# Block-diagonal queries: attention scores as full 128-row matmuls, with one layout buffer per mixer

## What is computed

```python
qa, ka, va, za, qb, kb, vb, zb, ga, gb = jnp.split(rms_norm(h, g_in) @ w_in, cuts, axis=-1)
# mixer A: 8 query heads, 2 key heads of 64; a chunk of 64 sees itself and the 2 chunks before
# mixer B: 8 query heads, 8 key heads of 64; a chunk sees itself and the 8 chunks before
s = jnp.einsum('bnqhgd,bnkhd->bnhgqk', qg, k) * (dh ** -0.5)
s = s + bias.reshape(Hkv, G, Cq, Kn)          # distance penalty (A) or learned table (B)
...                                           # mask, sink (A), softmax
o = jnp.einsum('bnhgqk,bnkhd->bnqhgd', pr, v)
branch_a = (oa * jax.nn.silu(za)) @ w_o_win
branch_b = (ob * jax.nn.silu(zb)) @ w_o_band
h = h + (jax.nn.sigmoid(ga) * branch_a + jax.nn.sigmoid(gb) * branch_b) @ w_out
gate = jax.nn.sigmoid(rms_norm(h, g_ple) @ w_ple_gate)
h = h + gate * (p @ w_ple)
```

## Time and profile before

| what | value |
|---|---|
| median of 3 runs | 1305.68 us (1210.99, 1305.68, 1320.73) |
| the profiled execution | 1209.5 us, span of the slowest core 1207.9 us |
| spans of the eight cores | 1203.1 to 1207.9 us |
| mean granted TensorE clock of the cores | 0.993 to 0.996 |
| busy: TensorE, VectorE, ScalarE, GpSimd | 96%, 60%, 54%, 39% of the span |
| DMA traffic of the slowest core | 106.84 MB, mean 88 GB/s |

### The profile page before, as it was taken

How to read it: one execution, slowest core, us unless ns; L and a number is a source line. 1 busy time by engine, 2 the same in 40 slices (tenths; PEclk the granted TensorE clock), 3 DMA queues, 4 the chain that set the end, 5 groups by cost and what they waited for, 6 DMA issues and landing times.

```text
span 1207.9 us, 22110 instructions; the slowest of 8 cores (1203.1 to 1207.9 us)
## 1 busy us (share of the span) xinstructions
PE 1156.1 (96%) x8119; PEld 569.9 (47%) x8275; DVE 723.9 (60%) x1671; ACT 650.8 (54%) x997; POOL 471.8 (39%) x516
## 2 busy tenths in 40 slices
PE   5799999999999999999999999999999999999896
PEld 2455554444444444444444444444444444444442
DVE  2765756556566655566566555565656556766654
ACT  2676554555555455555555555555555555655452
POOL 3743223433344433443444333443444334544520
PEclk9899999999999999999999999999999999999998
DMA  9999412333343334333443333333433344444463
GB/s 177 211 179 173 87 47 72 58 75 59 74 86 81 76 81 82 75 70 64 81 87 78 78 82 78 78 66 66 83 85 76 77 86 92 100 70 90 86 80 90
DMA packets 170252, 106.84 MB, mean 88 GB/s; under 512 B 149024, under 2 KB 154272, under 8 KB 167680
## 3 DMA queue, kind: packets, MB, share of 16 engines
q1 hardware_dynamic: 152608, 71.30, 25.6%
q0 software_dynamic: 17536, 34.12, 17.8%
HBM read 80.56 MB, written 21.50 MB: 84 GB/s over the span
## 4 chain that ended last, share of the span: by engine, by line
PE 91%; DMA 2%; DVE 2%; issue 2%; POOL 1%; ACT 1%; DVEq 0%; ACTq 0%; SPq 0%; POOLq 0%
PE psmm L203 81%; PE pss L203 6%; PE pso L203 5%; DMA xb<-xe 2%; POOL st L190 1%; DVE st L190 0%; DVE qkn L190 0%; DVE xb L190 0%; DVE psmm L190 0%; DVE scr L190 0%; DVE stq L190 0%; DVE ET L190 0%; DMA actT<-mbuf 0%; ACT ET L190 0%; ACT t1t L190 0%
## 5 line engine op out<-in xcount | busy, mean ns | idle before, releaser
L203 PE MATMUL psmm<-W_in,xT 128*128 128x512 bf16 (+1 forms) x2726 | 633.1, 370 | 11.8 <-issue 7.6
L203 PEld LDWEIGHTS psmm<-W_in,xT 128*128 128x128 bf16 x2848 | 251.7, 98 | 251.7 <-issue 12.0
L190 POOL TENSOR_TENSOR st<-st,mhalf 128x8 f32<-128x8 f32 (+1 forms) x174 | 227.6, 1313 | 164.5 <-DVE st L190 161.1
L190 ACT ACTIVATE ET<-pss 128x1024 bf16<-128x1024 f32 (+1 forms) x220 | 221.5, 1007 | 124.2 <-PE pss L203 122.1
L190 ACT ACTIVATE tg<-psmm,st 128x512 bf16<-128x512 f32 x132 | 90.1, 687 | 168.1 <-PE psmm L203 168.1
L190 POOL TENSOR_TENSOR zs<-ont,zs 128x256 bf16<-128x256 f32 (+1 forms) x132 | 89.5, 678 | 216.3 <-DVE ont L190 216.2
L203 PE MATMUL psmm<-W_pg,actT 128*128 128x512 bf16 x515 | 122.2, 386 | 4.9 <-DVE qkn L190 3.0
L203 PE MATMUL psmm<-W_out,actT 128*128 128x512 bf16 x521 | 120.3, 379 | 1.8 <-ACT actT L190 0.7
L190 ACT ACTIVATE scr<-psmm 128x512 f32<-128x512 f32 (+1 forms) x137 | 70.4, 517 | 66.3 <-PE psmm L203 44.9
L190 DVE TENSOR_TENSOR ET<-ET,tabAs 128x1024 bf16<-128x1024 bf16 (+1 forms) x66 | 44.8, 679 | 97.4 <-ACT ET L190 96.5
L190 DVE SCALAR_TENSOR_TENSOR psmm<-t1t,psmm 128x512 f32<-128x512 f32 x66 | 43.0, 693 | 94.5 <-PE psmm L203 94.5
(11 more groups left out here) (104 smaller groups left out, 1237.4 us busy)
## 6 DMA issues: line engine op xcount, KB each, us to landing
y<-xb SPq DMA_DIRECT2D x32, 512.0 KB, 2.6
xb<-xm SPq DMA_DIRECT2D x29, 512.0 KB, 3.9
W_in<-w_in POOLq DMA_DIRECT2D x10, 1024.0 KB, 27.0
xT<-xmT POOLq DMA_DIRECT2D x28, 256.0 KB, 3.9
xb<-xe POOLq DMA_DIRECT2D x2, 1536.0 KB, 13.6
pT<-pmT POOLq DMA_DIRECT2D x32, 64.0 KB, 2.4
W_out<-w_out POOLq DMA_DIRECT2D x2, 1024.0 KB, 63.0
W_pg<-w_pg POOLq DMA_DIRECT2D x2, 1024.0 KB, 59.2
```

Source lines behind the costliest of these rows:

```text
L190: inst = getattr(e, method)(*[_res(a_) for a_ in args], **{k_: _res(a_) for k_, a_ in kw.items()})
L203: last = getattr(e, m)(*[_res(a_) for a_ in a], **{k_: _res(a_) for k_, a_ in k.items()})
```

## The change

Queries are laid out block-diagonally. The staging area's columns 0 to 1023 are now shared by q of mixer A and q of mixer B, one after the other: each head pair takes 256 columns, of which the first and the last 64 hold the two heads and the 128 between them stay zero from one memset at the start. Transposed, a pair gives 128 partitions by 256 columns: one head on rows 0 to 63 of the first 128 columns, the other on rows 64 to 127 of the second 128, zeros elsewhere. With these the scores of two heads (mixer B) or four (mixer A) come from one matmul over all 128 rows of the key layout: mixer A has two of 512 columns, mixer B four of 256. qaT and qbT have 1024 columns and a single buffer each. Each mixer's q is transposed right after its multiply, so tiles on the TensorE path have 16 q blocks to transpose instead of 8. The order of heads in the exp buffers and in the tables changes with it, and at the start q of tile 1 is projected after the attention of tile 0 has been handed to the scheduler.

```diff
-    qaT = [sb(f"qaT{i}", [128, 512], BF16) for i in range(2)]
-    qbT = [sb(f"qbT{i}", [128, 512], BF16) for i in range(2)]
+    qaT = sb("qaT", [128, 1024], BF16)
+    qbT = sb("qbT", [128, 1024], BF16)
+    QR = ["qkn_q0", "qkn_q1"]
...
+    S.ins("dve", "memset", qkn[:, 0:1024], 0.0, w=QR, est=0.5)
...
-            o_ap = dst.rearrange("p (i kv d) -> p kv i d", kv=2, d=64)
-            i_ap = bank[:, c0:c0 + w].rearrange("p (kv i d) -> p kv i d", kv=2, d=64)
+            o_ap = dst.rearrange("p (i a d) -> p a i d", a=4, d=64)[:, 0:4:3]
+            pat = "kv i" if permute == "A" else "i kv"
+            i_ap = bank[:, c0:c0 + w].rearrange(f"p ({pat} d) -> p kv i d", kv=2, d=64)
...
+        def p_trq(dst_, dres):
             if t["dmaT"]:
-                for (off, w_, src_, dst_, dres) in (
-                        (0, 512, "qkn_qa", qaT[par][:], f"qaT{par}"), (1024, 128, "qkn_ka", kaT[:, sa, :], f"kaT{sa}"),
-                        (512, 512, "qkn_qb", qbT[par][:], f"qbT{par}"), (1152, 512, "qkn_kb", kbT[:, sbn, :], f"kbT{sbn}")):
-                    dmaT(dst_, qkn[:, off:off + w_], [src_], [dres])
+                dmaT(dst_[:], qkn[:, 0:1024], QR, [dres])
+                return
+            trx, trres = next_tr()
+            S.group("pe", [("transpose", (trx[:, c * 128:(c + 1) * 128], qkn[:, c * 128:(c + 1) * 128], ident[:]), {})
+                           for c in range(8)], r=QR + ["ident"], w=[trres])
+            S.ins("act", "copy", dst_[:], trx[:, 0:1024], r=[trres], w=[dres], est=1.0)
+
+        def p_trk():
+            if t["dmaT"]:
+                dmaT(kaT[:, sa, :], qkn[:, 1024:1152], ["qkn_ka"], [f"kaT{sa}"])
+                dmaT(kbT[:, sbn, :], qkn[:, 1152:1664], ["qkn_kb"], [f"kbT{sbn}"])
...
+                if "k" not in parts:
+                    bank, br = inproj_ct(t, 0, 512)
+                    qknorm(t, bank, br, 0, 8, qkn[:, 0:1024], QR, 0, permute="A")
+                    p_trq(qaT, "qaT")
+                if "Q" not in parts:
+                    p_a()
+                if "k" not in parts:
+                    bank, br = inproj_ct(t, 1280, 512)
+                    qknorm(t, bank, br, 0, 8, qkn[:, 0:1024], QR, 10, permute="B")
+                    p_trq(qbT, "qbT")
+                if "Q" not in parts:
+                    p_k()
+                    p_v()
+                    p_trk()
...
-                    sl = kt % RB_
-                    for hq in range(4):
-                        for hh in range(2):
-                            calls.append(("matmul", (ps_s[:, hh * 512 + hq * NQ:hh * 512 + (hq + 1) * NQ],
-                                                     kbT[hh * 64:(hh + 1) * 64, sl, hq * 128:(hq + 1) * 128],
-                                                     qbT[par][hh * 64:(hh + 1) * 64, hq * 128:hq * 128 + NQ]),
-                                          dict(start=True, stop=True)))
-                    S.group("pe", calls, r=[f"kbT{sl}", f"qbT{par}"], w=["pss0"], est=0.4)
+                sl = kt % (RA_ if mixer == "A" else RB_)
+                for g in range(2 if mixer == "A" else 4):
+                    nb_ = 4 if mixer == "A" else 2
+                    o_ = g * 512 if mixer == "A" else (g // 2) * 512 + (g % 2) * 2 * NQ
+                    lhs = kaT[:, sl, :] if mixer == "A" else kbT[:, sl, g * 128:(g + 1) * 128]
+                    rhs = (qaT if mixer == "A" else qbT)[:, g * nb_ * 128:(g + 1) * nb_ * 128]
...
+                    calls.append(("matmul", (ps_s[:, o_:o_ + nb_ * NQ], lhs, rhs), dict(start=True, stop=True)))
...
+                S.group("pe", calls, r=kr, w=["pss0"], est=0.45)
...
-    P(m[1], "q")
+    P(m[1], "qk")
     tabs_setup()
     P(m[0], "z")
     A(m[0])
+    P(m[1], "qQ")
     P(m[1], "z")
```

More of the change, by code:

```diff
@@ L605, in qknorm @@
         if permute:
-            o_ap = dst.rearrange("p (i kv d) -> p kv i d", kv=2, d=64)
-            i_ap = bank[:, c0:c0 + w].rearrange("p (kv i d) -> p kv i d", kv=2, d=64)
-            r_ap = rs.rearrange("p (kv i) -> p kv i", kv=2).unsqueeze(3).to_broadcast([128, 2, 4, 64])
-            S.ins("dve", "tensor_tensor", out=o_ap, in0=i_ap, in1=r_ap, op=ALU.mult, r=[bres, rsr], w=[dst_res],
+            o_ap = dst.rearrange("p (i a d) -> p a i d", a=4, d=64)[:, 0:4:3]
+            pat = "kv i" if permute == "A" else "i kv"
+            i_ap = bank[:, c0:c0 + w].rearrange(f"p ({pat} d) -> p kv i d", kv=2, d=64)
+            r_ap = rs.rearrange(f"p ({pat}) -> p kv i", kv=2).unsqueeze(3).to_broadcast([128, 2, 4, 64])
+            S.ins("dve", "tensor_tensor", out=o_ap, in0=i_ap, in1=r_ap, op=ALU.mult, r=[bres, rsr], w=dst_res,
                   est=0.15 + w / 950.0)
@@ L691, in p_tr @@
                 return
[L692 to L705, removed]
+            trx, trres = next_tr()
+            c_lo = 0 if needa else 1
+            S.group("pe", [("transpose", (trx[:, c * 128:(c + 1) * 128], qkn[:, 1024 + c * 128:1152 + c * 128], ident[:]), {})
+                           for c in range(c_lo, 5)], r=(["qkn_ka"] if needa else []) + ["qkn_kb", "ident"], w=[trres])
+            if needa:
+                S.ins("act", "mul", kaT[:, sa, :], trx[:, 0:128], gcol[:, 1:2], r=[trres, "gcol"], w=[f"kaT{sa}"], est=0.36)
+            S.ins("act", "mul", kbT[:, sbn, :], trx[:, 128:640], gcol[:, 3:4], r=[trres, "gcol"], w=[f"kbT{sbn}"], est=0.69)
         if "x" in parts:
@@ L714, in stage_P @@
                     p_a()
-                p_tr(True, False)
+                p_trk()
             else:
[L717 to L724, removed]
+                if "k" not in parts:
[11 more added lines that the diff above has]
+                    p_v()
+                    p_trk()
         if "z" in parts and full:
@@ L799, in stage_A @@
                 calls = []
-                if mixer == "A":
-                    sl = kt % RA_
-                    for hh in range(2):
[L803 to L807, removed]
-                    sl = kt % RB_
-                    for hq in range(4):
-                        for hh in range(2):
-                            calls.append(("matmul", (ps_s[:, hh * 512 + hq * NQ:hh * 512 + (hq + 1) * NQ],
-                                                     kbT[hh * 64:(hh + 1) * 64, sl, hq * 128:(hq + 1) * 128],
-                                                     qbT[par][hh * 64:(hh + 1) * 64, hq * 128:hq * 128 + NQ]),
-                                          dict(start=True, stop=True)))
-                    S.group("pe", calls, r=[f"kbT{sl}", f"qbT{par}"], w=["pss0"], est=0.4)
-                    tab, tres = tabB, "tabB"
+                sl = kt % (RA_ if mixer == "A" else RB_)
[4 more added lines that the diff above has]
+                    rhs = (qaT if mixer == "A" else qbT)[:, g * nb_ * 128:(g + 1) * nb_ * 128]
+                    if NQ < 128:
+                        rhs = heads(rhs)
+                    calls.append(("matmul", (ps_s[:, o_:o_ + nb_ * NQ], lhs, rhs), dict(start=True, stop=True)))
+                tab, tres = (tabA, "tabA") if mixer == "A" else (tabB, "tabB")
+                kr = [f"kaT{sl}", "qaT"] if mixer == "A" else [f"kbT{sl}", "qbT"]
+                S.group("pe", calls, r=kr, w=["pss0"], est=0.45)
                 units.append((E, eres, sl))
@@ L934, in stage_C @@
     def stage_C():
-        regions = [(0, "qkn_qa"), (512, "qkn_qb"), (1152, "qkn_kb"), (0, "qkn_qa")]
+        regions = [(0, "qkn_q0"), (512, "qkn_q1"), (1152, "qkn_kb"), (0, "qkn_q0")]
         for i in range(4):
@@ L974, in tabs_setup @@
                 S.ins("act", "activation", out=tabA[:, o_:o_ + 128], in_=stageA[:, rel * 128:(rel + 1) * 128],
-                      func=AF.Exp, scale=-(2.0 ** -(h + 1)), r=SA_, w=["tabA"], est=0.28)
+                      func=AF.Exp, scale=-(2.0 ** -((h % 2) * 4 + h // 2 + 1)), r=SA_, w=["tabA"], est=0.28)
     def pg_fold():
@@ L1141, in _make_in_maps @@
     rb = f(inp["rel_bias_band"])[0]
-    horder = [0, 2, 4, 6, 1, 3, 5, 7]
+    horder = list(range(8))
     tb = np.stack([rb[horder][:, idx0], rb[horder][:, idx1]], axis=0)
```

3 lines of the change are left out of this document (1 added, 2 removed).

## The result

The changed kernel's four runs took 1226.44, 1226.47, 1248.87 and 1250.76 us, median 1237.67; the two longer ones had two cores at a granted clock of 0.97 where the other six were at 0.99, and the ratios here, and the medians below, leave such runs out. Against the kernel before the ratio is **1.0131, 95% interval [1.0088, 1.0175]**, and 1.0137 [1.0123, 1.0152] when both were run again side by side (1226.62 against 1210.33 us). That is within 2%, which had a chance of 0.86, and 1226 lies inside the range of 1206 to 1236, but it is a loss of 16 us where 5.2 were forecast, and a time that the forecast's own range, 1208 to 1224, does not hold.

The account below looks back on a forecast made before the run. TensorE was taken to bound the kernel: 1209.5 us + 3.0 for scores + 2.2 for TensorE transposes = 1214.7, say 1215 us, everything else nothing. Own range 1208 to 1224; widened for parts of the rivals, 1206 to 1236.

Parts of the forecast that it names:

- The edges: Score groups on TensorE: 0.20 us of each split group's 0.42 is idle edges, which groups with 128 rows lose.
- The price of full rows: Scores on TensorE: twice the columns without edges adds 0.013 us to each of 231 groups, +3.0 us.
- Rival 1: Score groups: edges stay, made by the PSUM target or the semaphore; 48 us more, 1260 us; chance 0.05.
- The transposes on TensorE: Main tiles 0 to 3 and the sample tile: 16 q transposes instead of 8 each, +2.2 us.
- The DMA transposes: q transposes of 28 tiles: 1024 columns instead of 512, width nearly free, taken as nothing; bound 4.8 us to landing.
- The single qbT: Loop: qbT's issue moves behind the running tile's last mixer-B scores, with 16 to 18 us of slack; nothing.
- Rival 2: SyncE's queue: qbT's wait delays the actT transposes and TensorE waits 2.2 us a tile; 1276 or 1245 us; chance 0.09.
- The scheduler knows this dependence ... Nothing: SyncE's queue: the scheduler places qbT's issue after the scores rather than make the queue wait; cost nothing.
- The two ends. I take nothing: First and last tiles: later q copies and a second transpose round cost nothing; bounds +4.4 and -3 us.
- 0.3 us later: Loop, shared staging: mixer B's q multiply must wait for qaT's transpose to land, 0.3 us later; cost nothing.
- a new order whose period is not 34.2: Sign that would show the forecast wrong: a changed queue order giving a loop period other than 34.2 us.

Follow-up runs that it names:

- experiment 5: Changed kernel with half of each score matmul's query columns left out, so its results are wrong: 1189.66 us, ratio 0.9825 to the kernel before.
- split twin: Changed kernel with only the scores split again into 64-row matmuls: 1222.96 us with scheduler's cost 0.45, 1210.74 us with 0.40.
- experiments 3 and 4: Kernel before with the change's single buffers, shared staging and order, scores still split: 1217.18 us with scheduler's cost 0.40 (3), 1221.85 us with 0.45 (4).
- experiment 6: Kernel before with single qaT and qbT and the change's order, but two separate staging areas, split scores, cost 0.40: 1213.04 us, ratio 1.0021.
- experiment 2: Kernel before with only the scheduler's cost of a score group raised from 0.40 to 0.45 us: 1213.61 us, ratio 1.0027.
- experiment 8: Kernel before with only the scheduler's cost of a score group set to 0.39 us instead of 0.40: 1203.46 us, ratio 0.9944.

## Why the prediction was wrong, point by point

- **The edges: right. The price of full rows: ten times too high, in a small term.** 0.20 us of edges for each split group, none for the new ones (experiment 5, and the new rows beside the earlier trace rows); a group at 0.43 to 0.44. Rival 1 is out. The term of +3.0 us was mis-sized, though: the split group costs 0.436 us, not 0.42 to 0.425, with the 0.011 us that the matmul behind it takes longer, so 231 groups cost 0.3 us of work and not 3.0. That the times differ by 1.8 and 3.7 us with the order held fixed, around the 3.0 that were forecast, is luck: those are waits.
- **The transposes on TensorE: right in size.** 40 more of them (139 instead of 99 behind `qkn`), 40 x 0.056 = 2.2 us; with the scores TensorE's work grew by some 2 us instead of 5.2.
- **The DMA transposes: the size was off, without effect.** "Width seems nearly free" came from rows of 128 and 512 columns; 1024 columns took 3.1 us to land, not 2.4, within the bound of 4.8. SyncE's issue took 1.23 us.

```profile
qaT<-qkn SPq DMA_TRANSPOSE x28, 3.1
qbT<-qkn SPq DMA_TRANSPOSE x28, 3.1
```

- **The single qbT: right.** Its issue moved behind the last mixer-B scores, and behind kbT's, as the next rows show (SyncE's queue; the last score group of that tile starts at 606.17); the pair of actT<-mbuf stands ahead of it and waits for nothing of it. Rival 2 is out; TensorE waited for an actT<-mbuf once in the loop, 0.6 us.

```profile
603.76 2.93 SPq L190 DMA_TRANSPOSE actT<-mbuf  x2
606.75 1.24 SPq L190 DMA_TRANSPOSE kbT<-qkn  x1
608.20 1.23 SPq L190 DMA_TRANSPOSE qbT<-qkn  x1
```

- **"The scheduler knows this dependence ... Nothing": this step failed.** The diff shows `est=0.4` become `est=0.45`, and the working has no term for it. It took the planned order as a thing that can only adapt, while the loop's 34.12 us with no wait was the product of one such plan, and any edit of buffers or costs makes another. The sum treated a cost told to the planner as costless because it does no work. Its price is 14.0 us in the changed kernel, 12.2 in its split twin, 4.7 in experiments 3 and 4 and 3.3 in the kernel before: 6 of the 14 us by the wait for the exp and other waits of the loop, the greater part by the tail, whose change is measured but not explained.
- **"The two ends. I take nothing": this failed too, in size.** The bounds had +4.4 us, from ScalarE's copies. What came was a wait of another kind: the shared staging area puts the second q of tile 0 behind the first one's transpose, worth 6 us up to tile 6 and some 4 in the whole (experiment 6). For the loop that hand-over had been worked out ("0.3 us later"); for tile 0, where nothing covers it, it had not. In the tail, 4 us longer on the mean of the cores, the waits changed places and grew: 2.99 us for the q multiply in the earlier trace rows went, and instead TensorE waits three times for that multiply, 2.1 us, and for a load of cached keys, 1.7 us (the middle row was there before):

```profile
PE psmm L203 <- DVE qkn L190: 2.1, 3, 1.1
PE psmm L203 <- ACT actT L190: 1.8, 2, 1.1
PE psmm L203 <- DMA qkn<-ckb: 1.7, 1, 1.7
```

- **The range.** Its upper end, 1236, came from rival 2 and held the runs at 1226 only by that; "a new order whose period is not 34.2" stood among the things that would prove the forecast wrong, and had no chance of its own. It deserved one: with 0.38, 0.40 and 0.45 the same changed kernel runs at 1214, 1212 and 1227, and the kernel before with 0.39, 0.40 and 0.45 at 1203, 1210 and 1214.

What stays open: which decision of the scheduler makes the wait (that fewer PSUM banks are free at that place was not tested), and why the tails of the orders differ, by 5 us between 0.39 and 0.40 before and by 9 between 0.40 and 0.45 after the change. So it is shown that the order costs the time, and for the loop how; for the tail it is shown only that it does.

## What to carry to other kernels

Where a list scheduler writes the queues, a cost told to it is part of the change: price it as its own rival, with the spread that other values give, before the mechanism that was meant. Compare two ways of computing something with the order held fixed, and tune the number for each of them only after that; here the idea cost 2 to 4 us and the number 12 to 14. Price the edges of a split from the distance between whole periods, not from the group alone: a part of them stood in the matmul behind. And zeros in place of a row split are nearly free only where a split group is as short as here: 0.21 us of saved streaming against 0.21 of edges.

## What the runs showed of the hardware that was not expected

- A change from 128-row to 64-row matmuls costs 0.10 us (0.094 to 0.096), the way back 0.106, and the first 128-row matmul behind takes 0.011 us longer. With these, 512 columns side by side cost as much as 1024 in a row: 0.436 against 0.437 us for mixer B.
- A DMA transpose of 128x1024 bf16 lands 3.1 us after its issue, 0.7 later than one of 128x512, while the issue itself took 1.23 us of SyncE instead of 1.20.
- One gap of 2.79 us on TensorE near 52 us was followed, from 55 to 58 us on, by 3.4 to 6.8 us at the lower clock on all eight cores; the gaps of the kernel before there (1.1 us at most) and of the variant with two areas were not. No rule comes out of it: the same gap was not followed by it on core 7 of the changed kernel's second profile, on core 4 of experiment 3 and on four cores of experiment 5, and core 0 of experiment 2 and core 1 of experiment 8 had it behind gaps of 1.1 us at most.
